# Decoder step on one core: the first norm and its conditioning vectors worked out by halves of the channels, and a longer lead of tile 0 in the first MLP's first down unit

## What is computed

```python
mod = (silu(c) @ ada_w[i] + ada_b[i]).reshape(c.shape[0], 6, D)   # ada_w: 2 x 1024 x 6144
hn  = rmsnorm(x, norm_g[i, 0]) * (1 + mod[:, 1]) + mod[:, 0]       # scale is 1, shift is 0
out = mlstm_mixer(hn, ...)          # layer 0;  a gated short convolution in layer 1
x   = x + mod[:, 2] * out
hn  = rmsnorm(x, norm_g[i, 1]) * (1 + mod[:, 4]) + mod[:, 3]
x   = x + mod[:, 5] * (square(relu(hn @ w_up[i])) @ w_down[i])
```

## Time and profile before

| | before |
|---|---|
| median of 3 runs (lowest, highest) | 1310.14 us (1308.98, 1311.0) |
| the profiled execution: its time / the span of its records | 1309.41 us / 1307.7 us |
| PE, DVE, ACT, POOL busy | 97%, 59%, 39%, 28% of the span |
| granted TensorE clock, mean | 0.994 |

### The profile page before, as it was taken

One profiled execution on the slowest core, in us unless ns is written; L12 is line 12 of the kernel. 1 busy time (PEld: TensorE's weight loads), 2 busy tenths in 40 slices (PEclk: granted clock), 3 DMA queues, 4 the chain that ended last, 5 costly groups with the idle time before them and its releaser, 6 DMA issues.

```text
span 1307.7 us, 26354 instructions
## 1 busy us (share of the span) xinstructions
PE 1269.4 (97%) x11305; PEld 1243.4 (95%) x11305; DVE 772.1 (59%) x1296; ACT 504.7 (39%) x792; POOL 367.6 (28%) x184
## 2 busy tenths in 40 slices
PE   5799999999999999999999999999999999999996
PEld 4799999999999999999999999999999999999996
DVE  2623445667757643643659809859859743824764
ACT  3533453222532551551552322123362551642721
POOL 2434433443300041041044245435310041050050
PEclk9999999999999999999999999999999999999998
DMA  9667214754456574574553233323132242342321
GB/s 332 204 193 177 80 55 122 230 169 123 135 173 195 161 229 126 162 228 128 160 165 97 65 97 92 86 83 97 53 94 81 68 134 60 97 132 62 98 65 69
DMA packets 242526, 169.34 MB, mean 129 GB/s; under 512 B 5851, under 2 KB 217055, under 8 KB 242282
## 3 DMA queue, kind: packets, MB, share of 16 engines
q1 hardware_dynamic: 215946, 121.33, 32.4%
q10 hardware_dynamic: 26304, 46.27, 10.9%
q0 software_dynamic: 160, 0.07, 0.0%
HBM read 160.70 MB, written 6.94 MB: 128 GB/s over the span
## 4 chain that ended last, share of the span: by engine, by line
PE 80%; DVE 10%; issue 3%; DMA 3%; SPq 2%; ACT 2%; POOL 1%; POOLq 0%; DVEq 0%; ACTq 0%
PE G L1922 39%; PE G L2042 19%; PE G L1948 9%; PE G L2078 6%; PE B L2106 3%; SPq L462 1%; DVE hb L1396 1%; DMA raw<-in_mlp_w_down 1%; DVE small_s L1847 1%; DVE acc L1273 1%; DMA early<-in_ada_w 1%; PE B L1908 1%; DVE yc L1846 1%; DVE Xl L1410 1%; PE B L2290 1%
## 5 line engine op out<-in xcount | busy, mean ns | idle before, releaser
L1087 POOL TENSOR_TENSOR wl<-raw,wh 128x1024 fp32r<-128x1024 f32 x128 | 326.4, 2558 | 784.1 <-ACT wh L587 781.2
L587 ACT ACTIVATE wh<-raw 128x1024 fp32r<-128x1024 f32 x144 | 152.1, 1056 | 277.0 <-PE G L1922 147.4
L1922 PE MATMUL G<-Hh,wh 128*128 128x272 f32 x864 | 179.3, 289 | 0.0
L1922 PE MATMUL G<-Hh,wl 128*128 128x272 f32 x864 | 178.4, 288 | 0.0
L1922 PE MATMUL G<-Hl,wh 128*128 128x272 f32 x864 | 178.3, 288 | 0.0
L1922 PE MATMUL G<-Xh,wh 128*128 128x272 f32 x672 | 143.1, 294 | 1.0 <-POOL wl L1087 1.0
L1922 PE MATMUL G<-Xl,wh 128*128 128x272 f32 x672 | 138.7, 288 | 0.0
L1922 PE MATMUL G<-Xh,wl 128*128 128x272 f32 x672 | 138.3, 287 | 0.0
L1922 PEld LDWEIGHTS G<-Hh,wh 128*128 128x128 f32 x864 | 135.5, 188 | 1.0 <-issue 1.0
L1922 PEld LDWEIGHTS G<-Hl,wh 128*128 128x128 f32 x864 | 135.8, 189 | 0.0
L1922 PEld LDWEIGHTS G<-Hh,wl 128*128 128x128 f32 x864 | 135.0, 189 | 0.0
(11 more groups left out here) (385 smaller groups left out, 2732.0 us busy)
## 6 DMA issues: line engine op xcount, KB each, us to landing
raw<-in_mlp_w_up SPq DMA_DIRECT2D x64, 512.0 KB, 4.2
raw<-in_mlp_w_down SPq DMA_DIRECT2D x64, 512.0 KB, 4.4
aring<-in_ada_w ACTq DMA_DIRECT2D x60, 512.0 KB, 5.1
raw<-in_mlstm_w_in SPq DMA_DIRECT2D x24, 512.0 KB, 4.3
raw<-in_conv_w_in SPq DMA_DIRECT2D x24, 512.0 KB, 3.7
early<-in_ada_w SPq DMA_DIRECT2D x16, 512.0 KB, 12.2
free_l<-in_ada_w ACTq DMA_DIRECT2D x20, 256.0 KB, 6.8
raw<-in_mlstm_w_out SPq DMA_DIRECT2D x8, 512.0 KB, 4.7
```

What stands on the lines that cost most here:

```text
L587: nc.scalar.activation(wh[:, t % SLOTS], raw_of(t), ACT.Copy).then_inc(s_hi, 1)
L1087: nc.gpsimd.tensor_tensor(wl[:, t % SLOTS], raw_of(t), wh[:, t % SLOTS].bitcast(F32), ALU.subtract).then_inc(s_lo, 1)
L1922: last = mm(G[:, 2 * (g % 2) + hf, 0:HALF], w[:, s, k, :], x[:, k, hf * HALF:(hf + 1) * HALF], start=st, stop=en)
```

## The change

The two first vectors change places (scale first, then shift), and each is worked out in halves of the channels: SP fetches tiles 0 to 3 and 8 to 11, then the weights of tiles 0 and 1, then the other eight. PE does `ada_pair` 1, 4, 5; `gates(0)` to `gates(3)`; `ada_pair` 2, 3; steps k = 0..3 of tile 0; `ada_pair` 6, 7; steps k = 0..3 of tile 1; and for k = 4..7 the step of tile 0, that of tile 1, and `gates(k)`. The products of the shift go to the bank `B6`. DVE copies `rstd` to `xr` in SBUF, multiplies `xn` of four blocks, does transposes, bias, gain, samples and `Xl` of these four, and then the same of the other four. ACT does `hi(0)` and `hi(1)` behind k = 1 and k = 3, `hi(2)` and `hi(3)` behind k = 7. The lines after the gates' last product are unchanged on DVE and ACT. In the first MLP's first down unit the pair of tiles goes by `lagging(4)`.

```diff
-ADA_ORDER = (0, 1, 2, 4, 3, *range(5, 2 * NMOD))
+ADA_ORDER = (1, 0, 2, 4, 3, *range(5, 2 * NMOD))
+EARLY = (0, 1, 2, 3, 8, 9, 10, 11, 4, 5, 6, 7, 12, 13, 14, 15)
@@ SP
-            for a in range(2, ADA_RING):
+            for a in EARLY[2:8]:
                 ada_fetch(nc.sync, a)
             unit(T_QK, w_in, 0, order=range(RAWS))
+            for a in EARLY[8:]:
+                ada_fetch(nc.sync, a)
@@ ACT
+            def first_norm_hi(q):
+                ks = slice(4 * q, 4 * q + 4)
+                act.wait_ge(s_sm, q + 1)
+                for k in range(4 * q, 4 * q + 4):
+                    full = dict(bias=modT[:, 0, k, 0:1], scale=gain[:, k, 0:1])
+                    nc.scalar.activation(prompt(Xh[:, k, :]), prompt(xn[:, k, :]), ACT.Identity, **full).then_inc(s_hhi, 1)
+                    if k % 4 == 0:
+                        nc.scalar.activation(Xh[:, ks, :]..., samp[:, ks, :]..., ACT.Copy).then_inc(s_smh, 1)
+                    if k % 2:
+                        if k >= 2:
+                            act.wait_ge(s_kx, X_NORM0 + k - 1)
+                        nc.scalar.activation(prompt(hb[1][:, :]), prompt(xn[:, k, :]), ACT.Identity, **full).then_inc(s_hx, 1)
+                        if q == 0:
+                            hi(k // 2)
-            act.wait_ge(s_au, ADA_RING)
-            norm_hi(0, 0, 0)
+            first_norm_hi(0)
+            first_norm_hi(1)
+            hi(2)
             hi(3)
@@ DVE
+            def first_norm(q):
+                ks, gcol = slice(4 * q, 4 * q + 4), 96 + 4 * q
+                half = samp[:, ks, :].rearrange("p k (b t) -> p k b t", t=ST)
+                first_mod(0, q)      # waits s_au >= 8 * q + 4; transpose and bias of 4 channel blocks
+                chain.link(V.tensor_scalar(gain[:, ks, :], modT[:, 1, ks, :], 1.0, None, ALU.add))
+                chain.link(V.tensor_tensor(gain[:, ks, :], gain[:, ks, :], ..., ALU.mult))
+                chain.link(V.tensor_tensor(half, half, seq_cols(gain)[:, ks], ALU.mult))
+                first_mod(1, q)      # waits s_au >= 8 * q + 8
+                V.tensor_tensor(half, half, seq_cols(modT[:, 0])[:, ks], ALU.add).then_inc(s_sm, 1)
+            chain.link(V.tensor_copy(halves(xr[:, :]), rstd))
+            first_norm(0)
+            first_norm_low(0)
+            scaled_x(range(4, KT))
+            first_norm(1)
+            first_norm_low(1)
@@ PE
-            for k in range(1, 8):
+            ada_pair(1)
+            pe.wait_ge(s_xse, 1)
+            for k in (4, 5):
                 ada_pair(k)
...
-            gates(0)
-            gates(1)
+            for k in range(4):
+                gates(k)
+            ada_pair(2)
+            ada_pair(3)
+
+            def head_pair(t, g, xh, xl, j, per_t, per_g, ready):
+                def steps(k, o):
+                    if (k, o) == (3, 0):
+                        ada_pair(6)
+                        ada_pair(7)
+                    if k >= 4 and o == 1:
+                        gates(k)
+                order = (*((k, o) for o in range(2) for k in range(4)), *((k, o) for k in range(4, KT) for o in range(2)))
+                pair_steps(t, g, xh, xl, HALF, order, slots_drained(g), ready, steps)
...
-            tile_pair(T_MLP0 + 8, G_MLP0 + 8, Hh, Hl, None, 0, 0, drained(G_MLP0))
+            tile_pair(T_MLP0 + 8, G_MLP0 + 8, Hh, Hl, None, 0, 0, drained(G_MLP0), lagging(4))
```

More of the change, by code:

```diff
@@ L182, in build_program @@
         Xl = sb("Xl", [P, KT, TOK], F32R)
-        early1 = sb("early1", [P, 8, 2, QW], at=at_X)
+        early_x = [sb(f"early_x{i}", [P, 2, 2, QW], at=at_X + (8 * i + 4) * ROW) for i in range(2)]
         batch = sb("batch", [P, KT, 2, QW], at=at_X)
@@ L1330, in norm_samples_lo, with first_mod @@
[L1330 to L1333, removed]
+                dve.wait_ge(s_gn, n)
+            def first_mod(n, q):
+                d, ks = ADA_ORDER[n], slice(4 * q, 4 * q + 4)
+                dve.wait_ge(s_au, 8 * q + 4 * n + 4)
+                turned = V.transpose(adaT[:, 4 * n:4 * n + 4, :].rearrange("p m s -> p (m s)"),
+                                     (B4, B6)[n][:, P * q:P * (q + 1)])
+                if q:
+                    turned.then_inc(s_tr, 1)
+                    dve.wait_ge(s_tr, n + 1)
+                else:
+                    chain.link(turned)
+                added = V.tensor_tensor(modT[:, d, ks, :], adaT[:, 4 * n:4 * n + 4, 0:NSEQ],
+                                        par0[:, d * KT + 4 * q:d * KT + 4 * q + 4].unsqueeze(2).broadcast_to((P, 4, NSEQ)), ALU.add)
+                if q:
+                    added.then_inc(s_mod, 1)
+                    dve.wait_ge(s_mod, n + 1)
+                else:
+                    chain.link(added)
@@ new lines, in first_norm_low @@
+            def first_norm_low(q):
+                ks = slice(4 * q, 4 * q + 4)
+                for k in range(4 * q, 4 * q + 4):
+                    if k % 2 == 0:
+                        if k >= 2:
+                            dve.wait_ge(s_kx, X_NORM0 + k - 1)
+                        chain.link(V.tensor_scalar(prompt(hb[0][:, :]), prompt(xn[:, k, :]), gain[:, k, 0:1],
+                                                   modT[:, 0, k, 0:1], ALU.mult, ALU.add))
+                    if k % 4 == 0:
+                        dve.wait_ge(s_smh, q + 1)
+                        V.tensor_tensor(samples_of(Xl)[:, ks], samp[:, ks, :].rearrange("p k (h c) -> p k h c", h=2),
+                                        samples_of(Xh)[:, ks].bitcast(F32), ALU.subtract)
+                    if k % 2:
+                        dve.wait_ge(s_hx, k // 2 + 1)
+                    dve.wait_ge(s_hhi, k + 1)
+                    V.tensor_tensor(prompt(Xl[:, k, :]), prompt(hb[k % 2][:, :]), prompt(Xh[:, k, :].bitcast(F32)),
+                                    ALU.subtract).then_inc(s_kx, 1)
@@ L2084, in ada_pair @@
                 n, quad = k // 4, k // 2 % 2
-                if k % 4 == 0 and n:
+                if k % 4 == 0 and n >= 2:
                     pe.wait_ge(s_tr, n)
+                out = B6 if n == 1 else ada_out
                 for a in (2 * k, 2 * k + 1):
@@ L2123, in mixed @@
                     if m == 0 and ready is not None:
[L2124 removed]
+                        pair(t, g0, xh, xl, j, per_t, per_g, ready)
                     if m > 1 or ready is None:
@@ L2211, in post_k @@
                     last.then_inc(s_tt, 1)
-            mixed(T_QK, G_QK, 2, Xh, Xl, None, post=post_k, between=lambda m: (lambda k: gates(k + 2) if m == 0 and k + 2 < KT else None))
+            mixed(T_QK, G_QK, 2, Xh, Xl, x_ready(X_NORM0), post=post_k, pair=head_pair)
             def turn_keys(n):
```

87 lines of the change are left out of this document (33 added, 54 removed).

## The result

The changed kernel takes a median of 1313.55 us (10 runs, 1311.39 to 1314.69) against 1310.5 us for the kernel before (10 runs, 1308.98 to 1311.03): +3.05 us, a ratio of 1.0022 with a 95% interval of 1.0014 to 1.0030. That is inside the predicted range (1308.6 to 1314.4), on its slow side, and outside the range that the prediction gave to its forecast alone (1309.3 to 1312.5).

The account below looks back on a forecast made before the run. PE's matmul work bounds the kernel, so tile 2's start and clock and the MLP decide: +0.4 + 1.3 - 1.0 = +0.7 us, from 1310.14 to about 1310.9 us; range 1308.6 to 1314.4, the forecast's own 1309.3 to 1312.5.

Parts of the forecast that it names:

- signs of being wrong: No PE wait at tile 2, block 3's `Xl` lasting over 2 us, or the last gates outside 54 to 58.
- 7.6 us from the last gates to a free slot: Behind the last gates, DVE's and ACT's work until tile 0 leaves the slot that tile 2 needs: 7.6 us.
- PE idles 6.6 us in front of tile 2: Only 1.0 us of conditioning lies behind the last gates, so PE waits 6.6 us; tile 2 starts 0.4 us later.
- Rival 1, the lock: Block 3's `Xl`, issued after POOL's `lo(1)` begins, waits for all of it: +3.4 us, 1313.6; margin 0.22 us, chance 0.15.
- POOL 2.39 for `lo(0)` among transfers: In the head, POOL's `lo(0)` takes 2.39 us despite transfers; the earlier 2.73 was read as waiting for DVE.
- Samples out at 28.3: First half of the norm: PE's transposes of x end at 22.6, and the scaled samples are out at 28.3.
- What stood in front of the first gates before: In the old head: SP's last early transfer, issued at 22.34 and landed at 34.75, then transposes, gain and norm.
- The clock in the first gates: After PE's idle time from 25.4 to 30.5, a low clock in gates 2 and 3 and products behind: 0.4 us taken.
- From there to the last gates: PE's products from the end of gates 3 at 36.25 to 55.3, without another wait for the norm.
- The clock behind the stall: The idle time in front of tile 2 lowers the clock behind it: +1.3 us, bounds 0 and 2.6.
- The MLP pair: In the first MLP, PE's 0.97 us wait for tile 1's low weights goes: -1.0 us, bounds 0 and -1.0.
- rival 2: The clock stays low in the first gates until the conditioning products: last gates 57.5, +2.5 us, 1312.6; chance 0.12.

Follow-up runs that it names:

- evac_ahead: The changed kernel, but ACT moves tiles 0 and 1 out of `G` ahead of its wait for the gate rows, exp and log: 1304.62 us, ratio 0.9954 to the kernel before.
- lock: The changed kernel with `hi(1)` ahead of block 3's `hb`, so POOL's second `lo` comes before that block's `Xl`: 1316.85 us, ratio 1.0052 to the kernel before.
- before_evac: The kernel before, with ACT moving tiles 0 and 1 out of their slots ahead of its wait for the gate rows: 1310.18 us against 1310.38.
- mlp_only: The kernel before with only the change's MLP part, the first down unit's pair by `lagging(4)`: 1310.14 us against 1310.57.
- warm_stall: The changed kernel with 48 filler matmuls in PE's wait in front of tile 2: 1311.4 us, ratio 1.0003 to the kernel before.
- warm_start: The changed kernel with 30 fp32 filler matmuls in PE's wait for x at the start: 1316.89 us, ratio 1.0056 to the kernel before.
- warm_gates: The changed kernel with 34 filler matmuls in PE's idle time in front of the first gates: 1312.74 us, ratio 1.0020 to the kernel before.
- head_only: The changed kernel without its MLP part, that pair going by the old order: 1313.38 us, ratio 1.0026 to the kernel before.
- short_start: evac_warm with 18 fp32 filler matmuls ahead of PE's transposes of x at the start: 1303.83 us, ratio 0.9949 to the kernel before.
- evac_warm: evac_ahead with the 34 filler matmuls of warm_gates in front of the first gates: 1302.8 us, ratio 0.9950 to the kernel before.

## Why the prediction was right, and which terms were off

The mechanism was the one predicted: the change moves PE's idle time from the head to the front of tile 2, and nets to about nothing. The number was right less by the forecast than by the width of the range around it: 1313.55 lies past the forecast's own 1312.5, the ratio of 1.0022 lies just in the class "slower" (over 0.2%), which had a chance of 0.23, and one of the prediction's signs of being wrong came true: the last gates ended at 58.87, outside 54 to 58 and past the bound of 57.5. Point by point, in the profiled executions:

- *7.6 us from the last gates to a free slot*: 7.67 measured. *PE idles 6.6 us in front of tile 2*: 6.66, released by ACT's move out of `G`. evac_ahead shows that it is this, and nothing else, that keeps tile 2 back.
- *Rival 1, the lock*: not taken, with the margin as worked out (0.2 us). Kernel lock shows its price on top of the changed kernel: 3.9 us, where the rival gave 2.7; of the 3.9, 1.2 is the wait itself.
- *POOL 2.39 for `lo(0)` among transfers*: 2.38 at a DMA share of 1.05, and 2.69 where a DVE instruction was running. The choice between stretching and waiting was right.
- *Samples out at 28.3*: out at 30.14, **+1.8**. This is the term that was missed most. From the start of the 96 products to the samples are 5.79 us where the step has 5.7; what failed is the start itself. The step said that PE's transposes of x end "where its products start, 22.6", read from the earlier trace rows of one execution as if it were fixed. Here it was 24.35: x came 0.5 us later, the 20 transposes took 0.7 more, and spreading `rstd` 0.6 more. Over the eight kernels with the changed head that have no filler at the start, the 96 products begin anywhere from 22.39 to 24.35; over the three traces of the old head at 22.57, 22.81 and 22.75. Whether the change has a part in that, three traces against eight do not tell: in before_evac the transposes took 4.53 us too, with x landing at 14.27.
- *What stood in front of the first gates before*: the prediction names SP's last early transfer, landed at 34.75. In that trace PE waited for it for only 0.24 us, as its timeline shows:

```profile
34.80 0.65 PE L2106 MATMUL B<-early,cpad 128*32 128x128 f32 x16 [0.24 <-DMA early<-in_ada_w]
```

  In mlp_only and before_evac PE did not wait for it at all, and the chain runs from the landing of x through the transposes, `xn` and the products of the second vector, here in mlp_only:

```profile
30.15 5.23 PE B L2106 x128
```

  So the start of the head was already a quarter of a us from the chain, or on it; it was no slack that the change used up.
- *The clock in the first gates, 0.4 taken of 0 to 2.1*: about 1.35 us, since gates 2 and 3 ran from 36.61 to 39.44 where 1.5 us is full speed. **+0.95**. The bounds were right (0 to 2.2 over six executions) and the value taken was low for this one: the work behind the idle time had holes (1.52 us between gates 1 and 2), and the clock was not back until 39.
- *From there to the last gates*: 19.4 us for 19.05, +0.4, in the changes from one kind of product to the next. So the last gates ended at 58.87 instead of 55.7: 1.8 + 0.95 + 0.4.
- *The clock behind the stall, +1.3*: +1.55 (13.77 - 12.22), and warm_stall gets it back. Other executions with a stall of 6.65 us paid 1.8 to 2.1 (warm_start, warm_gates, lock, head_only).
- *The MLP pair, -1.0*: the 0.97 us wait is gone, but the stretch around it is only 0.5 us shorter (29.82 against 30.29), since PE then waits 0.52 us for the next conditioning weights. "PE sat idle for 0.97 us" was read as a gain of 0.97. **+0.5** against the forecast.

The sum of these: the forecast's +0.7, and 1.8 + 0.95 + 0.4 + 0.05 + 0.25 + 0.5 = 3.95 on top, 4.65 us, where the profiled executions differ by 4.6. The medians differ by 3.05, because the profiled execution of before was a short one for that kernel and that of after a long one for its own. Of the 3.05, some 2.4 us are therefore what the forecast missed, and the traces put most of it in two terms: the start of the head and the clock in the first gates. Both change from execution to execution, so how much each has in the medians is not shown. The second was the mechanism of rival 2, at half its size.

What stays open: why the head starts up to 2 us apart from execution to execution, and why the clock came back at 33 to 35 in one execution and at 39 in another; and the 4.5 us that warm_start lost near 285 us.

## What to carry to other kernels

Before a late transfer is called what holds an engine, look at how long the engine waited for it (0.24 us here) and at what came next to last: that path is what an edit uncovers. One trace shows one sample of its start, which lay anywhere in 2 us here. When work is moved earlier on one engine, look at what the other engines do between it and the next buffer that must come free: here two moves out of PSUM placed ahead of an exp and a log were worth 9 us, and nothing before the edit. An idle gap costs its length and the clock behind it (1.5 us here for a gap of 3.7, 1.55 to 2.1 for gaps of 6.7), and a removed wait of a microsecond is worth less than a microsecond until the next waits in line are known.

## What the runs showed that was not expected

- The clock stayed at the 1.2 GHz level from 33 to 39 us while PE was busy for 4.48 of the 6 us, with a gap of 1.52 in it. In short_start it fell in a wait of 2.28 us, which it outlived in evac_warm (2.3 us). What decides between the two, these runs do not show.
- The granted clock reads 1.00 from 16 to 20 us in every kernel without a filler there, while the same 20 transposes take 3.79 to 4.53 us, and 2.40 behind a filler. That a low clock is what made them slow is read from these durations alone; the column does not show it.
- A filler works in one place (warm_stall) and brings nothing or a loss in others (warm_gates, short_start, warm_start), though in all four the instructions right behind it ran at full speed.
